# Splitting GpSimd's slab subtraction into four pieces in a three-block transformer kernel

## The reference, cut to what matters

```python
xn = _rms_norm(h, mix_norm[l])
proj = xn @ w_in[l]                              # (512 x 1024) @ (1024 x several thousand)
...
merged = (jax.nn.sigmoid(gate_attn) * (y_attn @ w_branch_attn[l])
          + jax.nn.sigmoid(gate_rwkv) * (y_rwkv @ w_branch_rwkv[l]))
h = h + merged @ w_out[l]
hn = _rms_norm(h, ffn_norm[l])
gate, up = _split(hn @ w_gate_up[l], (FFN_HIDDEN, FFN_HIDDEN))
h = h + (jax.nn.silu(gate) * up) @ w_down[l]
```

## Time and profile before

| | |
|---|---|
| time, median of 3 runs | 3212.84 us (3211.89 to 3220.63) |
| the profiled execution | 3222.05 us, its span 3220.2 us |
| busy: PE / PEld | 2983.3 us (93%) / 2327.9 us (72%) |
| busy: DVE / ACT / POOL | 1420.0 us (44%) / 1157.7 us (36%) / 1194.8 us (37%) |
| L2761 alone | 442 instructions, 1095.6 us, mean 2481 ns |
| mean granted clock of TensorE | 0.954 of 2.4 GHz |

### The profile page before, as it was taken

One profiled execution on the slowest core, in us unless ns is written; L12 is line 12 of the kernel. 1 busy time (PEld: TensorE's weight loads), 2 busy tenths in 40 slices (PEclk: granted clock), 3 DMA queues, 4 the chain that ended last, 5 costly groups with the idle time before them and its releaser, 6 DMA issues.

```text
span 3220.2 us, 40009 instructions
## 1 busy us (share of the span) xinstructions
PE 2983.3 (93%) x15600; PEld 2327.9 (72%) x15600; DVE 1420.0 (44%) x2031; ACT 1157.7 (36%) x1680; POOL 1194.8 (37%) x557
## 2 busy tenths in 40 slices
PE   6989987979999999898999999987988987999998
PEld 5855646858888886767888887754866676788886
DVE  3007846455222373523365443334087652664442
ACT  4243352344222235333342223334353533542222
POOL 3422521124444452433544443411323322544442
PEclk9987988989999999999999999988999889999999
DMA  3322210033233332224422222311211102622222
GB/s 125 98 79 63 69 33 2 3 131 98 93 97 98 105 133 74 98 83 144 157 97 93 98 93 91 117 47 48 87 59 68 70 22 76 215 97 93 98 93 84
DMA packets 80667, 284.07 MB, mean 88 GB/s; under 512 B 8968, under 2 KB 9096, under 8 KB 79744
## 3 DMA queue, kind: packets, MB, share of 16 engines
q1 hardware_dynamic: 66240, 236.36, 22.1%
q10 hardware_dynamic: 13296, 41.97, 3.4%
q0 software_dynamic: 976, 3.56, 0.4%
HBM read 260.86 MB, written 20.99 MB: 88 GB/s over the span
## 4 chain that ended last, share of the span: by engine, by line
PE 38%; issue 36%; POOL 15%; DVE 7%; ACT 3%; DMA 1%; POOLq 0%; SPq 0%; ACTq 0%; DVEq 0%
POOL slab_r L2761 15%; PE bank L345 10%; PE bank L347 9%; PE bank L346 9%; PE bank L566 2%; DVE work L2220 1%; PE bank L452 1%; PE bank L543 1%; DVE small L2218 1%; DVE work L2207 1%; PE bank L620 1%; PE bank L899 1%; PE bank L462 0%; DVE work L2530 0%; PE bank L633 0%
## 5 line engine op out<-in xcount | busy, mean ns | idle before, releaser
L2761 POOL TENSOR_TENSOR slab_r<-slab,slab_high 128x1024 fp32r<-128x1024 f32 x442 | 1095.6, 2481 | 1684.6 <-ACT slab_high L1133 1684.5
L345 PE MATMUL bank<-xh,slab_high 128*128 128x512 f32 x2256 | 906.0, 402 | 30.4 <-POOL slab_r L2761 21.4
L347 PE MATMUL bank<-xh,slab_r 128*128 128x512 f32 x2256 | 886.5, 393 | 0.0
L346 PE MATMUL bank<-x_raw_r,slab_high 128*128 128x512 f32 x2064 | 812.9, 394 | 0.0
L1133 ACT CAST slab_high<-slab 128x1024 fp32r<-128x1024 f32 x442 | 462.3, 1047 | 455.0 <-DMA slab<-in_w_down 216.1
L346 PE MATMUL bank<-work_r,slab_high 128*128 128x512 f32 x1376 | 545.9, 397 | 0.0
L345 PEld LDWEIGHTS bank<-xh,slab_high 128*128 128x128 f32 x2256 | 429.8, 190 | 140.7 <-issue 26.4
L345 PE MATMUL bank<-work_r,slab_high 128*128 128x512 f32 x1184 | 472.7, 399 | 51.6 <-DVE work_r L1960 25.0
L347 PEld LDWEIGHTS bank<-xh,slab_r 128*128 128x128 f32 x2256 | 428.9, 190 | 93.2
L347 PE MATMUL bank<-work_r,slab_r 128*128 128x512 f32 x1184 | 473.4, 400 | 0.0
L346 PEld LDWEIGHTS bank<-x_raw_r,slab_high 128*128 128x128 f32 x2064 | 393.9, 191 | 80.8 <-issue 1.7
(11 more groups left out here) (464 smaller groups left out, 2868.8 us busy)
## 6 DMA issues: line engine op xcount, KB each, us to landing
slab<-in_w_down SPq DMA_DIRECT2D x88, 512.0 KB, 3.2
slab<-in_w_up SPq DMA_DIRECT2D x64, 512.0 KB, 3.2
slab<-in_w_gates SPq DMA_DIRECT2D x56, 512.0 KB, 3.3
slab<-in_w_merge SPq DMA_DIRECT2D x48, 512.0 KB, 3.8
slab<-in_w_gu SPq DMA_DIRECT2D x44, 512.0 KB, 3.5
slab<-in_w_in_a SPq DMA_DIRECT2D x32, 512.0 KB, 3.5
gates<-staging ACTq DMA_DIRECT2D x56, 256.0 KB, 2.2
slab<-in_w_out SPq DMA_DIRECT2D x24, 512.0 KB, 3.3
```

The lines of the kernel that those rows point to most:

```text
L345: first = pe.matmul(bank[b][:, :], wh, mh, start=start, stop=False)
L346: pe.matmul(bank[b][:, :], wh, ml, start=False, stop=False)
L347: end = pe.matmul(bank[b][:, :], wl, mh, start=False, stop=stop)
L2761: pool.tensor_tensor(slab_low[:, slot, :], slab[:, slot, :], plain(slab_high[:, slot, :]), ALU.subtract).then_inc(S("slab_split"), 1)
```

## The change

The one subtraction of 1024 columns becomes four of 256 columns each, of the same slot, in order. The first one is preceded by the same wait as before; only the fourth raises `slab_split`, so TensorE still waits for the whole slab. Nothing else differs. GpSimd issues 1326 more instructions.

```diff
                         pool.wait_ge(S("slab_high"), i * RING + (s0 + j + 1))
-                        pool.tensor_tensor(slab_low[:, slot, :], slab[:, slot, :], plain(slab_high[:, slot, :]),
-                                           ALU.subtract).then_inc(S("slab_split"), 1)
+                        for q in range(4):
+                            at = slice(q * SLAB * P // 4, (q + 1) * SLAB * P // 4)
+                            low = pool.tensor_tensor(slab_low[:, slot, at], slab[:, slot, at],
+                                                     plain(slab_high[:, slot, at]), ALU.subtract)
+                            if q == 3:
+                                low.then_inc(S("slab_split"), 1)
```

## The result

The changed kernel takes 3199.24 us (median of 5 runs, 3196.94 to 3202.22). The kernel before, run beside it, takes 3218.08 (5 runs, 3211.89 to 3220.63). The ratio is 0.9947, with an interval of 0.9932 to 0.9961: faster by 0.5%, or 18.8 us. The forecast was 3211.3, "within 0.3%", and its range began at 3202. Nearest to it is rival 2 (-15 us, 3198), which had 16%. The forecast was set against 3212.84, the median of three runs; the median of five is 5.2 us higher, so it is the differences that should be compared: -1.5 us forecast, -18.8 measured.

A forecast was written before the change was run, and what follows sets the result against it. TensorE, 93% busy, was taken as the bound, so its waits count. Costs of 5.4 us less gains of 6.9 (start 0.9, attention 6) gave -1.5 on the median 3212.84, thus 3211.3 us; range 3202 to 3224.

The forecast's parts named there:

- rival 2: VectorE's waits are worth more: attention returns all 8.1 us plus 3.3 of low clock, small wins elsewhere; -15 us, 3198, 16%.
- What bounds, and the port: Whole kernel: TensorE, 93% busy, bounds it; some VectorE operations wait at a shared port until GpSimd's current instruction ends.
- A quarter and a slab: GpSimd's subtraction: a quarter takes 0.747 us, four take 2.87 against 2.40 whole, so +0.47 us a slab.
- +0.47: Extra us per undisturbed slab, booked as cost at TensorE's waits at 1337.12, 1511.42 and 2043.83, 1.4 us together.
- A contended slab of 4.4 us: Beside dense VectorE work, turns of 1.21 us alternate, so a slab takes 4.4 us instead of 2.35: +2.0 us.
- rival 1: VectorE keeps the port for several operations, so five tight slabs come up to 4.3 us later each; +14, 3227 us, 12%.
- The costs on TensorE's path, 5.4 us: At TensorE's waits for slabs: 1.4 us at three uncontended ones, +2.0 each at 2458.49 and 2718.62.
- grows by about 2: In the scan, TensorE's wait at 1302.86 lengthens by about 2 us, offset by its 5.34 us idle before 1337.12.
- The start, -0.9: At the kernel's start, L1892 waits until 19.06 instead of 19.94, and the first matmul inherits the 0.9 us.
- Attention, -6: In attention, L2207's nine waits fall from 11.7 to 3.6 us, freeing 8.1 on VectorE; three quarters counted, -6 us.
- VectorE wins nothing there: In dense VectorE chains, four quarters delay VectorE about 0.5 us each, against 2.1 before, so no gain.
- rival 4: New low clock: idle times at 1511 and before 2043 grow, two clock drops cost 6.6 us; 3218 us, 10%.

The follow-up runs named there:

- uneven: Against the kernel before: four subtractions per slab of 32, 32, 32 and 928 columns instead of one of 1024; 3221.78 us, ratio 1.0014.
- all_but_attention: Against the kernel before: four pieces for every slab except those made during attention, which stay whole; 3208.62 us, ratio 0.9975.
- before_again: The kernel before, unchanged, run and profiled a second time; 3218.3 us, ratio 1.0006.
- after: The changed kernel itself, four pieces of 256 columns per slab, against the kernel before; 3199.24 us, ratio 0.9947.
- attention_only: Against the kernel before: four pieces only for the slabs made during attention, one piece elsewhere; 3208.51 us, ratio 0.9973.
- the halves: Two runs against the kernel before: four pieces only for slabs made during attention (9.1 us faster), and four everywhere but there (9.0 faster).
- after_again: The changed kernel, unedited, run and profiled a second time against the kernel before; 3197.33 us, ratio 0.9942.
- l2207_accum: Against the kernel before, slabs still in one piece: L2207 also writes out a row sum that nobody reads; 3211.31 us, ratio 0.9976.

## Why the prediction was wrong, step by step

**What bounds, and the port: right.** TensorE is 93% busy before and after. The hold's length is what VectorE waits for (uneven shows it by taking the gain away with the same number of instructions).

**A quarter and a slab: right.** Predicted 0.747 us and 2.87; measured 0.742 at the median and 2.81 undisturbed, so +0.41 instead of +0.47. The Trainium skill (GPSIMD Engine Reference, section Elementwise — side-by-side cycle accounting) had led to an estimate of +0.2 for a slab; the measurement decides against it.

**A contended slab of 4.4 us: right in kind.** Measured 4.80 in the scan, 3.86 at slab 329, 4.50 at 352, 4.24 at 285. The turns come one for one, so rival 1 (VectorE keeps the port) did not occur.

**The costs on TensorE's path, 5.4 us: near in size, not in every place.** In all_but_attention TensorE loses 0.4 us at slab 186, 1.5 at 329 and 2.7 at 352 and 353 (1.8 of waiting and 0.9 of a longer low clock behind it), 4.6 in all. It loses another 1.3 at slab 321, which was not on the list, and has it back at slab 322. Slabs 156 to 158 in the scan cost 2.5, given back at slab 163, as "grows by about 2" and "nothing" said; but there the wait fell from 5.34 to 1.23, more than was lent, since the scan ended earlier. At slab 286 (2043.83) the subtraction did end 0.49 later against L1952's end, as "+0.47" said, but the wait itself fell from 3.33 to 0.17 since slab 285 had become late. The clock stayed up behind slab 286 and fell behind 285: 2.5 us gained from slab 283 to 287 where a cost was booked. L2763's waits sum to 24.4, not "about 28".

**The start, -0.9: right and worthless.** The first matmul starts at 19.78 (19.7 predicted), but slab 1 starts 0.3 us later than before.

**Attention, -6: right for the waits, but without the clock.** Predicted was that L2207 gives 8.1 us on VectorE, of which three quarters count. It gives 7.1 to 8.6 (all 32 together take 27.8 us in the first profile before and 29.2 in before_again, 20.6 in after). TensorE's idle time from slab 32 to 47 is 5.1 to 6.4 us less in attention_only, so the -6 holds for it, though the factor of three quarters had no row behind it beyond TensorE's idle share. The timing of attention_only is 9.1: the low clocks of this stage are the term that the sum put at nothing and gave to rival 2. The sign "idle in 266 to 436 some 6 us less" read 2.5 in after, where more of the gain is clock. "L2207 never above 1.2 us" was off as well: its longest is 1.447.

**"VectorE wins nothing there": the step that failed.** The turn of 1.21 us was right (4.80 for four), but from it I took a wait of about 0.5 us a quarter, made four of them equal to one whole wait of 2.1, and so booked every dense chain as cost only. Measured are 0.36 to 0.42 us a quarter (0.75 to 1.11, 0.49 to 0.85, 0.69 to 1.11), 1.4 to 1.7 for four. So a dense chain gains on every slab that it meets: the scan takes 35.6 us instead of 37.4, the normalization 14.7 instead of 16.5. All but attention was to cost 5.4-0.9 = 4.5 us; it gave 9.0. That is 13.5 of the 16.6 us by which the sum was off (-1.5 against the halves' -18.1); attention is the other 3.1. The gain is small at each slab, but it is had at every chain on which TensorE waits: against the first profile before, all_but_attention's has TensorE 3.0 us further ahead across the scan (slabs 49 to 164), 5.3 across the normalization (164 to 178), 2.5 from 283 to 287 and 3.4 from there to 304. Of the 5.3, 1.7 came ahead of slab 175; they are absent in after and present in before_again, so they are the scatter of the clock and not the change. Against before_again's profile the first two figures are 4.2 and 3.4.

**Rival 2: near in total, not in its parts.** It gave attention 8.1+3.3 us and "small wins in the other mixers" the 3.6 that were left to 15. Measured are 9.1 and 9.0. That its total is within 4 us of the result is in part luck.

**The clock: a term that was missing.** In the first profile before, waits of TensorE of 2.28, 5.34 (slab 163), 2.97 and 3.33 us were each followed by a low clock that cost 3.0, 1.4, 1.9 and 2.8 us. All four waits fell (to 0, 1.22, 1.21 and 0.17), and all four low clocks went. In exchange new ones came: 1.6 us behind slab 285, 0.9 more behind 352, and 1.5 behind 186 in after, though not in after_again. I weighed new low clocks (rival 4) and the loss of one old one (rival 2), but never listed which existing waits were followed by a low clock. At the last three places wait and low clock went together in all fourteen profiles: waits of at most 1.3 us with full clock behind them, waits of 2.1 us or more with a low one. At the first place they did not: of three profiles with the wait, two have the low clock. None of the eleven without it does. Slab 163, before and after:

```profile
1337.12:1343.00 5.88, 5.88 (x20) 4.77 (x21) 0.00 (x0) 0.29 (x1) 4.53 (x2) 0.75 0.24 89
```

```profile
1314.32:1320.00 5.68, 5.68 (x25) 4.72 (x26) 0.00 (x0) 0.35 (x1) 5.43 (x8) 1.00 0.25 92
```

**What stays open.** What lets the clock in 229 to 266 come out at 0.64 or 0.95, and behind the same wait of 2.3 us in attention at 0.51 or 1.00; that second choice is the 3 us that all_but_attention's profile gained from slab 35 to 36, where that kernel is as before. The 5 us in l2207_accum are open too. How the whole gain divides between waits and clock in an average execution is therefore not shown, only that both begin with VectorE's waits for long subtractions.

## What to carry to other kernels

Where GpSimd and VectorE meet at the port, price the wait at both lengths of the hold for every chained VectorE operation, not only at the few places where TensorE is seen waiting for that operation; the busy time of VectorE's groups over their own shortest duration gives the most that there is to win. It is an upper bound: L2005 alone had 112 us of it and lost 82, at places where TensorE was not waiting for it. Cut the GpSimd operation only so far that a slab, each piece with its turn of VectorE's, stays shorter than TensorE's use of it (4.8 against 5.4 us for four, 6.2 for eight). Look at each wait of TensorE that is followed by a low clock: shortening it can give back both, and a slab made faster ahead of a fixed wait can lose both.

## What the runs showed of the hardware

The two engines alternate one instruction each when both always have a contending one ready, and a GpSimd quarter then costs VectorE 0.36 to 0.42 us and not its whole 0.74. Extra instructions cost GpSimd little: an undisturbed slab takes 2.81 us in four pieces against 2.40 in one, 0.14 us a piece. The tensor_scalar that also writes out an accumulator was not held up by GpSimd in any of its 32 executions (0.346 to 0.348 us for 128 columns and 0.746 to 0.749 for 512, beside 2.4 us subtractions). Its price is a longer time by itself (0.49 us for 512 columns without the accumulator) and 84 ns for the read of the accumulator. TensorE's idle time of 1.22 us ahead of slab 163 in after was followed by full clock; that of 2.01 us ahead of slab 285 in after by a mean clock of 0.71, and those of 2.28 and 2.97 us in the kernel before by 0.51 and 0.82, in the stretches shown. One and the same place can go either way. After an idle time of 2.40 us, 16 matmuls of L452 in the normalization took 8.80 us before and 8.61 in after, but 7.11 in all_but_attention, where the idle time was 2.39. After 2.38 us ahead of slab 158 its 24 matmuls took 7.16 us in before, and after 2.39 us 5.74 in before_again. Such places scatter the time of a single execution by some 1.7 us each, and a difference that rests on one of them alone is no result.
